# First norm of a fused two-block transformer kernel split into a latent half and a context half, with its input and table transfers in another order

## The reference

```python
silu_c, silu_cc = silu(c), silu(c_ctx)
m = split(silu_c @ w_ada[0] + b_ada[0], 6)             # sh1, sc1, g1, sh2, sc2, g2
h = modulate(rms_norm(lat, g_norm1[0]), sh1, sc1)      # latents
csh1, csc1, ... = split(silu_cc @ w_ada[0] + b_ada[0], 6)
hc = modulate(rms_norm(cx, g_norm1[0]), csh1, csc1)    # context
mix, _ = even_mixer(h, hc, w_in_even[0], ...)          # q, k, v, u, z = h @ w_in ; kc, vc = hc @ w_in[k, v columns]
def rms_norm(x, g): return x * rsqrt(mean(x * x) + EPS) * g
def modulate(h, shift, scale): return h * (1 + scale) + shift
```

## Time and profile before

| | us |
|---|---|
| median of 3 runs | 2724.62 |
| lowest, highest of the runs | 2718.01, 2727.05 |
| span of the profiled execution | 2724.3 |
| PE busy | 2547.2 (93%) |
| DVE busy | 1125.1 (41%) |
| ACT busy | 482.0 (18%) |
| bytes read from memory | 771.35 MB, 285 GB/s over the span |

### The profile page before, as it was taken

One profiled execution on the slowest core, in us unless ns is written; L12 is line 12 of the kernel. 1 busy time (PEld: TensorE's weight loads), 2 busy tenths in 40 slices (PEclk: granted clock), 3 DMA queues, 4 the chain that ended last, 5 costly groups with the idle time before them and its releaser, 6 DMA issues.

```text
span 2724.3 us, 39998 instructions
## 1 busy us (share of the span) xinstructions
PE 2547.2 (93%) x16144; PEld 1860.4 (68%) x16144; DVE 1125.1 (41%) x2652; ACT 482.0 (18%) x1042; POOL 225.3 (8%) x266
## 2 busy tenths in 40 slices
PE   6999999899999998999999779999999999999998
PEld 3565545557667765667666346669899866798998
DVE  1455114321112143110011241667687716676876
ACT  2132013221111022000000121431200114312101
POOL 0000000000000000000011000002122100020221
PEclk9989999999999999999999889999999999999999
DMA  9868999999997678999999962414544544245440
GB/s 405 341 255 360 420 410 415 418 398 412 418 418 302 278 299 347 419 419 418 418 415 417 420 244 109 143 69 180 233 170 159 212 171 143 83 166 215 157 155 17
DMA packets 121782, 779.74 MB, mean 286 GB/s; under 512 B 13248, under 2 KB 16960, under 8 KB 37888
## 3 DMA queue, kind: packets, MB, share of 16 engines
q1 hardware_dynamic: 94976, 684.76, 62.2%
q0 software_dynamic: 22560, 82.32, 7.8%
q10 hardware_dynamic: 4064, 10.09, 1.0%
HBM read 771.35 MB, written 5.77 MB: 285 GB/s over the span
## 4 chain that ended last, share of the span: by engine, by line
PE 78%; DMA 11%; DVE 8%; ACT 2%; issue 1%; SPq 0%; ACTq 0%; DVEq 0%
PE bank L726 76%; DMA ring<-in_stream 10%; PE bank L1149 1%; DMA work<-in_stream 1%; DVE MX L2387 1%; PE bank L730 1%; DVE work L2406 1%; DVE work L2289 1%; DVE bank L2389 0%; SPq L585 0%; DVE X L2328 0%; ACT work L1804 0%; DVE A L2994 0%; DVE work L2993 0%; DVE A L2995 0%
## 5 line engine op out<-in xcount | busy, mean ns | idle before, releaser
L726 PE MATMUL bank<-A,work 128*128 128x128 f32 (+1 forms) x2864 | 511.8, 329 | 12.4 <-DMA work<-in_stream 8.0
L726 PE MATMUL bank<-A,ring 128*128 128x128 f32 (+1 forms) x3088 | 508.1, 316 | 14.7 <-ACT A L1814 5.8
L726 PEld LDWEIGHTS bank<-A,work 128*128 128x128 f32 x2864 | 444.1, 193 | 72.3 <-issue 34.9
L726 PEld LDWEIGHTS bank<-A,ring 128*128 128x128 f32 x3088 | 449.6, 193 | 57.1 <-issue 12.2
L726 PE MATMUL bank<-work 128*128 128x128 f32 (+2 forms) x2704 | 402.3, 319 | 23.3 <-ACT work L1705 8.0
L726 PE MATMUL bank<-ring,A 128*32 128x512 f32 (+3 forms) x2272 | 366.2, 611 | 30.7 <-DMA ring<-in_stream 29.1
L726 PEld LDWEIGHTS bank<-work 128*128 128x128 f32 (+1 forms) x2704 | 319.6, 177 | 82.4 <-issue 38.0
L726 PE MATMUL bank<-work,ring 128*128 128x128 f32 (+1 forms) x1696 | 295.3, 323 | 1.6 <-DVE work L2410 1.6
L726 PEld LDWEIGHTS bank<-ring,A 128*32 128x32 f32 (+2 forms) x2272 | 116.6, 124 | 259.0 <-issue 203.3
L726 PEld LDWEIGHTS bank<-work,ring 128*128 128x128 f32 x1696 | 260.1, 194 | 22.0 <-DVE work L2410 2.1
L677 POOL DMA_DIRECT2D work<-in_stream x148 | 80.0, 541 | 1304.7 <-PE bank L726 1209.6
(11 more groups left out here) (334 smaller groups left out, 1918.0 us busy)
## 6 DMA issues: line engine op xcount, KB each, us to landing
ring<-in_stream SPq DMA_DIRECT2D x652, 1024.0 KB, 15.5
work<-in_stream POOLq DMA_DIRECT2D x140, 512.0 KB, 9.0
spill<-work ACTq DMA_DIRECT2D x6, 512.0 KB, 8.6
work<-in_stream POOLq DMA_DIRECT2D x8, 384.0 KB, 7.8
work<-spill POOLq DMA_DIRECT2D x6, 512.0 KB, 5.0
X<-in_xt ACTq DMA_DIRECT2D x1, 2048.0 KB, 13.3
work<-spill POOLq DMA_DIRECT2D x2, 768.0 KB, 11.8
tab_sb<-in_tab_a ACTq DMA_DIRECT2D x1, 1120.0 KB, 9.5
```

The lines of the kernel that those rows point to most:

```text
L726: return pay(pe.matmul(o, w, x, start=start, stop=stop, tile_position=place), tells)
```

## The change

The norm of the first layer becomes two: `n1_0` for the latents, `n1_0c` for the context, each at 256 columns.

- ACT issues only the latent half of `xt` at the start. The context half is issued when the modulation rows are done (`mod_raw`), `tab_a` after the latents' shifts, `WSP` and `ctx2t` after the context's shifts. `xt` keeps its layout in memory, so each of the two transfers takes 256 floats (1 KB) out of every 512.
- PE does the latents' sums at 256 columns where the sums at 512 stood, and the context's sums, into bank 5, between query groups 1 and 2. `even_k` waits for the context half of `A`, chunk by chunk.
- DVE takes the latents' reciprocal before it waits for the modulation rows, scales the latents' eight chunks, and makes the context's gain after that. Between query groups 1 and 2 it takes the context's reciprocal and scales the context's eight chunks.

The core of the diff:

```diff
             mod_rows(0)
-            norm("n1_0", 2 * T)
+            norm("n1_0", T)
...
                        wait=normed("n1_0") if j == 0 else None)
+                if j == 1:
+                    norm("n1_0c", T, sums=5)
             used()
             for n in range(4, 7):
                 mod_rows(n)
-            linear("even_k", 0, 2 * T, lambda k: tile("even", 32 + k), lambda k: A[:, k, :], KD)
+            linear("even_k", 0, 2 * T, lambda k: tile("even", 32 + k), lambda k: A[:, k, :], KD,
+                   wait=normed("n1_0c"))
...
-            act.dma_start(X[:, :, :], xt).then_inc(x_in, 16)
+            act.dma_start(X[:, :, 0:T], xt[:, :, 0:T]).then_inc(x_in, 16)
...
             act.wait_ge(x_in, 16)
-            act.dma_start(tab_sb[:, 0:N_TA], tab_a).then_inc(taba_in, 16)
-            act.dma_start(WSP, wsp_d).then_inc(wsp_in, 16)
             act.wait_ge(eps_ready, 1)
...
-            squares("n1_0", 2 * T, lambda k: X[:, k, :])
-            shifts("n1_0", lambda k: A[:, k, :], [(0, T, lambda k: mod(0, 0, k, 0)), (T, 2 * T, lambda k: mod(0, 0, k, 1))])
+            squares("n1_0", T, lambda k: X[:, k, 0:T])
+            act.wait_ge(mod_raw, 1)
+            act.dma_start(X[:, :, T:2 * T], xt[:, :, T:2 * T]).then_inc(ctx_in, 16)
+            shifts("n1_0", lambda k: A[:, k, 0:T], [(0, T, lambda k: mod(0, 0, k, 0))])
+            act.dma_start(tab_sb[:, 0:N_TA], tab_a).then_inc(taba_in, 16)
+            act.wait_ge(ctx_in, 16)
+            squares("n1_0c", T, lambda k: X[:, k, T:2 * T], sums=5, std=RSTD2)
+            shifts("n1_0c", lambda k: A[:, k, T:2 * T], [(0, T, lambda k: mod(0, 0, k, 1))])
+            act.dma_start(WSP, wsp_d).then_inc(wsp_in, 16)
             act.dma_start(X[:, :, T:2 * T], ctx2t).then_inc(ctx2_in, 16)
...
             dve.wait_ge(par_in, 16)
+            root("n1_0")
             dve.wait_ge(mod_raw, 1)
             mod_copy(0)
             take_mods(0, 0, 0, 0, 4)
-            gain(0, 0, 8, 0, par_("g1", 0, KD))
-            link(gain(1, 0, 8, 1, par_("g1", 0, KD)))
-            norm("n1_0", 2 * T, lambda k: X[:, k, :], lambda k: A[:, k, :],
-                 [(0, T, lambda k: GSC[:, 0, k:k + 1]), (T, 2 * T, lambda k: GSC[:, 1, k:k + 1])])
-
+            link(gain(0, 0, 8, 0, par_("g1", 0, KD)))
+            for k in range(KD):
+                dve.scalar_tensor_tensor(A[:, k, 0:T], X[:, k, 0:T], GSC[:, 0, k:k + 1], RSTD, ALU.mult, ALU.mult).then_inc(mid_ready, 1)
+            gain(1, 0, 8, 1, par_("g1", 0, KD))
             for j in range(4):
+                if j == 2:
+                    dve.wait_ge(ctx_in, 16)
+                    norm("n1_0c", T, lambda k: X[:, k, T:2 * T], lambda k: A[:, k, T:2 * T],
+                         [(0, T, lambda k: GSC[:, 1, k:k + 1])], RSTD2)
                 dve.tensor_scalar(QRAW[:, j, :], take("even_q", j, T), 0.125, None, ALU.mult).then_inc(taken["D"], 1)
```

More of the change, by code:

```diff
@@ L162 @@
 LIN_BANKS = 4
-NORMS = ["n1_0", "n2_0", "n1_1", "n2_1", "final", "ln_in",
+NORMS = ["n1_0", "n1_0c", "n2_0", "n1_1", "n2_1", "final", "ln_in",
          "cq0", "ckv0", "ln1_0", "ln2_0", "cq1", "ckv1", "ln1_1", "ln2_1"]
@@ L360, in build_program @@
         ident, ones, before = par_("ident"), par_("ones"), par_("before")
-        SQ, MEAN, RSTD, RSTD2 = wk(15360, 2, 512), wk(16128, T), wk(16896, T), wk(14336, 2 * T)
+        SQ, MEAN, RSTD, RSTD2 = wk(15360, 2, 512), wk(16128, T), wk(16896, T), wk(14336, T)
         QRAW, QK, KV_K = wk(0, 5, T), wk(1280, 5, T), wk(2560, 2 * T)
@@ L431, in build_program @@
         cX, cA = X[:, :, T:2 * T], A[:, :, T:2 * T]
-        par_in, x_in, taba_in, tabb_in, wsp_in = (sem(n) for n in ("par_in", "x_in", "taba_in", "tabb_in", "wsp_in"))
+        par_in, x_in, ctx_in, taba_in, tabb_in, wsp_in = (sem(n) for n in ("par_in", "x_in", "ctx_in", "taba_in", "tabb_in", "wsp_in"))
         ctx2_in, out_sent = sem("ctx2_in"), sem("out_sent")
@@ L1059, in seven, with norm @@
                     used()
-            def norm(name, w, mean=False):
+            def norm(name, w, mean=False, sums=6):
                 K, base = NCHUNK[name], NBASE[name]
@@ L1068, in norm @@
                     pe.wait_ge(sq_ready, base + k + 1)
-                    mm(bank[6][:, 0:w], ones, SQ[:, (base + k) % 2, 0:w], k == 0, k == K - 1, tells=True).then_inc(sq_used, 1)
+                    mm(bank[sums][:, 0:w], ones, SQ[:, (base + k) % 2, 0:w], k == 0, k == K - 1, tells=True).then_inc(sq_used, 1)
             def stats(name, j, K):
@@ L1790, in beside, with squares @@
                 side(thread, slot)
-            def squares(name, w, x, mean=False, come=None):
+            def squares(name, w, x, mean=False, come=None, sums=6, std=RSTD):
                 base, dim, eps = NBASE[name], NCHUNK[name] * P, 0 if name[:2] in ("n1", "n2", "fi") else 1
@@ L1805, in squares @@
                 act.wait_ge(sq_used, base + NCHUNK[name])
-                act.activation(RSTD if w == T else RSTD2, bank[6][:, 0:w], ACT.Sqrt, bias=EPS[:, eps:eps + 1], scale=1.0 / dim)\
+                act.activation(std, bank[sums][:, 0:w], ACT.Sqrt, bias=EPS[:, eps:eps + 1], scale=1.0 / dim)\
                    .then_inc(std_ready, 1)
@@ L2283, in beside, with root, norm @@
                 side(thread, slot)
-            def root(name, w):
+            def root(name, r=RSTD):
                 dve.wait_ge(std_ready, NSTAT[name] + 1)
-                r = RSTD if w == T else RSTD2
                 link(dve.reciprocal(r, r))
                 return r
-            def norm(name, w, x, out_, halves):
-                r = root(name, w)
+            def norm(name, w, x, out_, halves, r=RSTD):
+                r = root(name, r)
                 for k in range(NCHUNK[name]):
@@ L2331, in spread @@
                 even(1)
-                root(name, T)
+                root(name)
                 for k in range(KD):
```

## The result

| | before | changed |
|---|---|---|
| median | 2723.46 us (4 runs, 2718.01 to 2727.05) | 2742.50 us (4 runs, 2733.26 to 2745.05) |
| span of the profiled execution | 2724.3 us | 2741.9 us |

The changed kernel is slower by 0.7%, 19 us by the medians: ratio 1.007, interval 1.005 to 1.0089. The forecast was 2742.

A forecast was written before the change was run, and what follows sets the result against it. PE was taken as the chain from the first query on, so delay at the keys is kept. Waits for latents and context in 1 KB pieces put the keys 17.8 us later: 2724.3 + 17.8 = 2742.1, forecast 2742 us, range 2730 to 2752.

The forecast's parts named there:

- rows 1 to 3 end: Modulation rows on PE after the latents' sums end at 38.0: 5.36 us for three rows, ending at 43.3.
- keys start: PE's arrival at the keys, the measuring point: 82.5 us instead of 64.7, 17.8 us later.
- Rate of the small pieces: ACT's queue beside the strips' queue: 46 packets of 1 KB per us, so 22.3 us for 1024 packets.
- From landing to the first sum: Latents' landing to PE's first sum: 2.0 us instead of 3.0, less two DMA issues and part of a square.
- Query group 0: First query group on PE: 5.6 us, between 3.5 at the full clock level and 6.9 at the lower.
- Context: Context's transfer issued at 43.3, first data at 47.4, landed at 63.4 us; PE stands before its sums from 56.0.
- `ctx2t`: Second context's transfer, issued at 76: again 22.6 us, landing near 102, before DVE wants it at 103; nothing added.
- Keeping the loss: After the keys: the 17.8 us of delay there stays constant and is found again at the end.
- The base: Whole kernel: the delay is added to the profiled execution's span before, 2724.3 + 17.8 = 2742.1 us.
- both transfers take the full time: Rival, chance 0.13: context lands at 70.4, its sums end at 77.3, keys at 89.5, +24.8 us, 2749.
- The one by bytes: Rival, chance 0.10: small pieces get about half the bytes, latents land at 12.5, keys at 57.6, net -5 us, 2719.
- only the latents' transfer bites: Rival, chance 0.15: strips' ring runs dry before the context's transfer, which lands before 56; keys at 73.1, +8.4 us, 2733.

The follow-up runs named there:

- two-plane version: The changed kernel with X and its input laid out as two planes, so each half comes in 8 KB pieces, order untouched: 2717.97 us against 2723.93, ratio 0.9976.

## Why the prediction was right

The forecast was 2742, the median 2742.5. The mechanism was right: the cut of `xt` into 1 KB pieces, each with one turn against 8 KB of a strip. The versions with 8 KB pieces remove the holes one by one, and the cut alone puts one into the kernel before. That the figure fits to half a microsecond is luck: the four runs spread from 2733 to 2745, several terms were off, and some of it cancelled:

| | forecast | measured |
|---|---|---|
| latents landed | 30.0 | 28.3 |
| sums of the latents | 32.0 to 38.0 | 28.87 to 34.8 |
| rows 1 to 3 end | 43.3 | 40.1 |
| first query | 47.0 | 43.66 |
| query group 1 ends | 56.0 | 50.8 |
| context landed | 63.4 | 62.5 |
| sums of the context | 64.3 to 70.3 | 63.10 to 69.0 |
| keys start | 82.5 | 81.11 |

- **Rate of the small pieces.** I took 46 per us from the earlier trace rows, 1012 packets in 22 us. That stretch runs past the end of the transfer: only some 10 of its pieces moved after 72 us. From 52 to 70 us, in the same trace:

```profile
q1 hardware_dynamic: 888, 6.44, 86.9%
q10 hardware_dynamic: 905, 0.92, 15.1%
```

  That is 50 per us, and the changed kernel has the same from 9 to 27 us:

```profile
q1 hardware_dynamic: 906, 6.52, 87.6%
q10 hardware_dynamic: 902, 0.92, 15.0%
```

  So the latents needed 1.7 us less, and the trace of before could have told it.
- **From landing to the first sum.** I took 2.0 us, with ACT's table load in it. It took 0.6: with the two DMA issues out of the way nothing in front of the load waits for X any more, and it ran at 7.80 us, long before. I had read only that two issues went. The version that asks for the context earlier shows the same from the other side: with an issue in that place again, the load ran at 28.71, after the landing. These two terms are 3.1 of the 3.2 us by which the rows ended early.
- **Query group 0.** I took 5.6 us, expecting the lower clock. It took 3.6; the granted clock was 1.00, the full level, from 43.60 to 47.20, after PE had been busy without a hole from 28.87 to 40.1 and had then stood 0.97 and 1.54 us. In the two-plane version, where PE had waited for strips at 24.5 and 26.9 us, it was 0.50, the lower level, from 31 to 36 us around the start of that group. No run changes this alone.
- **Context.** Asked for 3.1 us earlier than forecast, it landed only 0.9 earlier, 22.4 us after its issue and not 20.1. Its first piece moved at 44.2, as long after the issue as I had it. From there the strips still had 5.7 MB to fetch and not 5.3, about 1.0 us more. The other 1.3 us are in the tail: the strips had all but ended at 60.0, yet the context's last 200 pieces took until 62.0, the last of them beside pieces of `tab_a`, where I had the rest come alone in 1 us. So the earlier arrival of PE mostly became a longer wait, 12.26 us instead of 8.3. This is why the errors ahead of it, 5.2 us by query group 1, left 1.4 at the keys.
- **`ctx2t`.** I had it take 22.6 us again. It took 6.5: it was asked for at 75.06, before the strips that row 4 sets free (from 75.83), and went alone, as the early context did for its last part. It was off the path either way. `tab_a` was held back behind the context as said (19.3 us) and nobody waited.
- **Keeping the loss.** 16.4 us at the keys, 16.2 at the rows after `z`, 17.6 at the end. The last 1.4 lie within what executions of one kernel differ by, and I leave them open.
- **The base.** I set the sum, 2742.1, against the span. A run's time lies 1.8 us above its span (2743.7 for 2741.9), which I left out; the median of before happened to stand at its profiled span. This is part of the luck.

Of the rivals, *both transfers take the full time* had as one ground that `xt` is cut in memory too; a cut in memory took no longer than a cut in `X` (27.7 us against the 27.1 of `ctx2t`). The one by bytes was worked out for a kernel that the layout then made real: keys at 57.6, strip 16 at 99.8, 2719. Measured in the two-plane version: 57.82, 99.33, 2718.0. That the ring would run dry and let the context through ("only the latents' transfer bites") is what happened when it was asked for at 28 us.

## What to carry to other kernels

Ask of every transfer that is split, delayed or moved how long its contiguous pieces become and what else is queued at that time. Beside the stream of large pieces here a transfer's time went by its count of pieces, not its bytes, so half a tensor in sixteenths of the piece size came later than the whole. Keep a tile that is to be fetched in halves as planes, and lay out its source in memory the same way: with one of the two still cut, the pieces stay small. Where the transfers are full up to some point, look there for how much of a gain ahead of it can be kept.

## What the runs showed of the hardware

That two queues share the engines by pieces I had from the trace of before. Counted over all packets, the turns are one for one: 906 of the strips' queue beside 902 of ACT's from 9 to 27 us of the changed kernel, 888 beside 905 from 52 to 70 us before. In the first of these stretches 111 packets are under 512 B, nearly all of them on the strips' queue, and the equal totals say that they take turns too. So 901 pieces of 1 KB went beside only 796 of 8 KB.

A transfer of 1 MB in 1 KB pieces took 27.7, 22.4, 12.3 or 6.5 us from issue to landing, by what lay in the other queue. Alone, the pieces are not slow: from 78 to 80 us of the changed kernel `ctx2t` moved 715 of them, 0.73 MB or some 366 GB/s, against 411 to 418 GB/s with the strips full.

While the strips' queue was full, a transfer on ACT's queue moved its first piece about 4 us after its issue (40.16 to 44.2 in the changed kernel, 47.41 to 51.2 for `ctx2t` before). With both queues empty it was 0.9 us (`WSP` in the changed kernel, issued at 74.69, first piece at 75.6).
